# Smaller first modulation blocks, token tiles normed one by one, and a store's wait two tiles later, in a diffusion-trunk kernel

## The reference, cut to what matters

```python
mod = jax.nn.silu(cond) @ w_mod[l] + b_mod[l]          # cond = c_ctx or c; w_mod is 1024 x 6144
shift1, scale1, gate1, shift2, scale2, gate2 = jnp.split(mod, 6, axis=-1)
h = _rms_norm(x, g_pre_mix) * (1 + scale1) + shift1    # per token, over 1024 features
proj = jnp.einsum('bld,de->ble', h, w_in)              # 1024 -> 512 q, 128 k, 128 v, 512 gu, 512 gv
```

## Time and profile before

| | |
|---|---|
| median of 3 runs | 643.16 us (642.53 to 644.21) |
| profiled execution | 639.3 us |
| its span, first to last instruction | 637.4 us |
| TensorE busy | 539.1 us (85% of the span) |
| VectorE, ScalarE, GpSimd busy | 182.9, 150.7, 175.4 us |
| moved by the DMA engines | 173.21 MB, mean 272 GB/s |

### The profile page before, as it was taken

How to read it: one execution, slowest core, us unless ns; L and a number is a source line. 1 busy time by engine, 2 the same in 40 slices (tenths; PEclk the granted TensorE clock), 3 DMA queues, 4 the chain that set the end, 5 groups by cost and what they waited for, 6 DMA issues and landing times.

```text
span 637.4 us, 10100 instructions
## 1 busy us (share of the span) xinstructions
PE 539.1 (85%) x3527; PEld 308.3 (48%) x3527; DVE 182.9 (29%) x572; ACT 150.7 (24%) x375; POOL 175.4 (28%) x242
## 2 busy tenths in 40 slices
PE   0689999999989999999997899899997878878700
PEld 0644684454575664555553465565653434434300
DVE  1311160001348871344466211111111101111026
ACT  2511031012127870322221111112111111111133
POOL 1100000014404441344444333243333223320214
PEclk9999999999997999999996999999999888999955
DMA  8999626070499602441194999999999999999278
GB/s 295 360 369 386 229 66 229 0 263 1 139 257 408 256 2 95 169 166 64 50 347 156 343 407 407 406 408 402 400 398 401 382 400 394 406 408 407 84 310 199
DMA packets 57091, 173.21 MB, mean 272 GB/s; under 512 B 5756, under 2 KB 7476, under 8 KB 56128
## 3 DMA queue, kind: packets, MB, share of 16 engines
q1 hardware_dynamic: 48512, 153.76, 63.9%
q0 software_dynamic: 7184, 15.70, 7.8%
q10 hardware_dynamic: 1328, 2.87, 1.1%
HBM read 163.75 MB, written 16.68 MB: 283 GB/s over the span
## 4 chain that ended last, share of the span: by engine, by line
PE 54%; DMA 35%; DVE 4%; SPq 2%; issue 2%; ACT 1%; POOL 1%; POOLq 0%; ACTq 0%; DVEq 0%
DMA ring<-in_w_down_dram 15%; PE ps L746 11%; PE ps L639 11%; PE ps L518 7%; PE ps L596 5%; DMA w_6d<-in_w_down_dram 5%; PE ps L893 4%; PE ps L537 4%; DMA ring<-in_w_mod_dram 3%; PE ps L621 3%; PE ps L698 3%; DMA w_7d<-in_w_down_dram 3%; DMA w<-in_w_down_dram 3%; PE ps L723 2%; DMA ring<-in_w_up_dram 2%
## 5 line engine op out<-in xcount | busy, mean ns | idle before, releaser
L893 PE MATMUL ps<-ring,xt 128*64 128x256 f32 x704 | 83.6, 391 | 15.4 <-DMA ring<-in_w_up_dram 10.4
L893 PEld LDWEIGHTS ps<-ring,xt 128*64 128x64 f32 x704 | 55.4, 140 | 49.7 <-DMA ring<-in_w_up_dram 16.6
L639 PE MATMUL ps<-ring,h_t 128*128 128x512 f32 x160 | 69.5, 593 | 0.0
L1407 DVE TENSOR_TENSOR hid<-act_g,ps 128x128 f32<-128x128 f32 x32 | 9.2, 288 | 195.7 <-ACT act_g L1635 195.7
L893 PE MATMUL ps<-w,xt 128*64 128x256 f32 x416 | 50.9, 400 | 9.9 <-DMA w<-in_w_up_dram 7.9
L746 PE MATMUL ps<-ring,mix_t 128*128 128x512 f32 x120 | 53.6, 596 | 0.0
L1762 POOL DMA_INDIRECT expert_results<-y_sb,idx_out x32 | 32.7, 1021 | 60.3 <-ACT y_sb L1649 51.0
L893 PEld LDWEIGHTS ps<-w,xt 128*64 128x64 f32 x416 | 33.6, 144 | 31.6 <-DMA w<-in_w_up_dram 12.2
L639 PEld LDWEIGHTS ps<-ring,h_t 128*128 128x128 f32 x160 | 30.1, 190 | 36.8 <-issue 36.8
L1693 POOL TENSOR_TENSOR gm_stats<-gm_stats,half_pow 128x8 f32<-128x8 f32 x5 | 9.7, 1941 | 124.4 <-DVE gm_stats L1129 124.4
L1753 POOL DMA_INDIRECT xg<-h_rows,idx_in x32 | 33.4, 1043 | 28.2 <-POOL idx_in L1751 22.7
(11 more groups left out here) (242 smaller groups left out, 728.4 us busy)
## 6 DMA issues: line engine op xcount, KB each, us to landing
ring<-in_w_mod_dram SPq DMA_DIRECT2D x12, 2048.0 KB, 15.3
ring<-in_w_gate_dram SPq DMA_DIRECT2D x20, 1024.0 KB, 9.4
ring<-in_w_up_dram SPq DMA_DIRECT2D x20, 1024.0 KB, 14.2
ring<-in_w_down_dram SPq DMA_DIRECT2D x20, 1024.0 KB, 16.4
w<-in_w_gate_dram SPq DMA_DIRECT2D x12, 1024.0 KB, 8.3
w<-in_w_up_dram SPq DMA_DIRECT2D x12, 1024.0 KB, 13.5
y_back<-expert_results SPq DMA_DIRECT2D x5, 1024.0 KB, 9.0
ring<-in_w_in_dram SPq DMA_DIRECT2D x2, 2048.0 KB, 18.7
```

The source lines that it names most:

```text
L639: last = pe.matmul(ps[:, 4 + u % 4, :], h_t[:, k, i * P:(i + 1) * P], w[:, k, :], start=(k == 0), stop=(k == KC - 1))
L893: last = pe.matmul(bank[fh * SLOT:(fh + 1) * SLOT, 0:FE].rearrange("p (a f) -> p a f", a=2), x_t[:, k % 4, (k // 4) * SLOT:(k // 4 + 1) * ...
```

## The change

The first two blocks are cut anew: `m0` now has chunks 0 and 1 of both `shift1` and `scale1` (two transfers of 256 columns), and `m1` chunks 2 and 3 of both. So `m0` alone gives what query chunks 0 and 1 need. SyncE loads tile 0 and latent tile 1 first, then `cst`, the other tiles, `cst_once`, `m0`, the first half of the query weights, and only then `m1`. Means, `pow` and scaling go tile by tile, GpSimd doing five `pow` of one column; VectorE scales tiles 0, 1 and 2, ScalarE 3 and 4. Tiles 0, 1 and 2 are turned ahead of `m0`, and `m1` moves behind query chunk 0. The cached keys, cached values, sink logits and router weights are loaded by GpSimd after the query projection's end, beside the gating weights that it used to load after the last `turn_tokens`; the cached keys are turned in the `gv` stage. ScalarE waits for the stores of `new_k` and `new_v` at tile 2 instead of at tile 0.

```diff
-MB_FIRST = [0, 8, 4, 12] + list(range(16, N_MOD * KC, MB_CHUNKS))
+MB_PARTS = [[(0, 2), (8, 2)], [(2, 2), (10, 2)], [(4, 4)], [(12, 4)]] + [
+    [(j, 4)] for j in range(16, N_MOD * KC, MB_CHUNKS)]
...
+        DVE_CHUNKS, ACT_CHUNKS = [0, 2, 4, 5], [1, 3, 6, 7]
...
+            sp.dma_start(res[:, 0, :], x_prompt[0]).then_inc(s_xp, 16)
+            sp.dma_start(res[:, 1, :], x_lat[:, 0]).then_inc(s_xp, 16)
             sp.dma_start(cst[:], consts[:, 0:N_KEPT]).then_inc(s_const, 16)
+            sp.dma_start(res[:, 2:TILES, :], x_lat[:, 1:]).then_inc(s_xs, 16)
             sp.dma_start(cst_once[:], consts[:, N_KEPT:]).then_inc(s_const, 16)
-            sp.dma_start(res[:, 0, :], x_prompt[0]).then_inc(s_xp, 16)
-            sp.dma_start(res[:, 1:TILES, :], x_lat).then_inc(s_xs, 16)
...
             load_mod(0)
+            load_in("q", 0, ATT, slice(0, KC // 2), wide_in[place("q")])
             load_mod(1)
-            load_in("q", 0, ATT, slice(0, KC // 2), wide_in[place("q")])
...
-            pe.wait_ge(s_rows, 144)
-            transpose(ps[:, 3, 256:256 + N_ROWS], rows[:, :], N_ROWS)
-            transpose(ps[:, 3, 128:256], cache_sb[:, :]).then_inc(s_colps, 1)
-            pe.wait_ge(s_silu, 2)
+            pe.wait_ge(s_rows, 128)
+            transpose(ps[:, 3, 256:256 + N_ROWS], rows[:, :], N_ROWS).then_inc(s_colps, 1)
...
+            for i in range(3):
+                turn_tokens(i)
+            pe.wait_ge(s_silu, 2)
             mod_block(0)
-            turn_tokens(0)
+            turn_tokens(3)
             mod_turn(0)
-            turn_tokens(1)
-            mod_block(1)
-            turn_tokens(2)
-            mod_turn(1)
-            for i in range(3, TILES):
-                turn_tokens(i)
+            turn_tokens(4)
...
             queries(0, range(TILES))
-            queries(1, range(TILES))
+            mod_block(1)
+            queries(1, range(2))
+            mod_turn(1)
+            queries(1, range(2, TILES))
             mod_block(2)
...
                 mod_turn(5)
+                pe.wait_ge(s_cv, 48)
+                pe.wait_ge(qk_dve, TILES)
+                transpose(ps[:, 3, 128:256], cache_sb[:, :]).then_inc(s_colps, 1)
...
+            mean_token(2)
+            tokens_out(0)
+            mean_token(3)
+            scaled_token(2)
+            tokens_out(1)
+            mean_token(4)
+            tokens_out(2)
             mod_cols(0)
-            tokens_out(0)
+            tokens_out(3)
             mod_sum(0)
-            tokens_out(1)
+            tokens_out(4)
+            pre_mix(0)
             mod_cols(1)
-            tokens_out(2)
             mod_sum(1)
-            for i in range(3, TILES):
-                tokens_out(i)
-            pre_mix_half(0)
+            pre_mix(1)
...
                 if i == 2:
-                    act.wait_ge(s_newkv, 16)
+                    act.wait_ge(s_newkv, 32)
...
                     act.dma_start(new_v[0, 0].rearrange("s h d -> s (h d)"), v_all[:, 5, :]).then_inc(s_newkv, 16)
-                    act.wait_ge(s_newkv, 32)
...
+            for i in range(TILES):
+                pool.wait_ge(s_ms1, i + 1)
+                rsqrt(stats[:, 7, i:i + 1], stats[:, 1, i:i + 1], 1, s_rs1)
+
+            pool.wait_ge(ht_tr, TILES)
+            pool.wait_ge(qkv_mm, 1)
+            pool.dma_start(cache_sb[:, :], cache_k[0, 0].rearrange("s h d -> s (h d)")).then_inc(s_cv, 16)
```

More of the change, by code:

```diff
@@ L979, in _, with mean_token, scaled_token @@
             link(dve.memset(ones_b[:], 1.0))
+            def mean_token(i):
+                dve.wait_ge(s_sq1, i + 1)
+                dve.tensor_scalar(stats[:, 1, i:i + 1], stats[:, 0, i:i + 1], 1.0 / D, EPS, ALU.mult,
+                                  ALU.add).then_inc(s_ms1, 1)
+            def scaled_token(i):
+                dve.wait_ge(s_rs1, i + 1)
+                dve.tensor_scalar(res[:, i], res[:, i], stats[:, 7, i:i + 1], None, ALU.mult).then_inc(xn_dve, 1)
+            mean_token(0)
+            mean_token(1)
+            scaled_token(0)
+            dve.wait_ge(s_colps, 1)
+            dve.tensor_copy(cols[:], ps[:, 3, 256:256 + N_ROWS]).then_inc(s_cols, 1)
+            dve.wait_ge(s_cols, 1)
+            scaled_token(1)
             dve.wait_ge(s_const, 32)
@@ L1006, in mod_sum @@
                 dve.wait_ge(mod_tr, b + 1)
-                j0 = MB_FIRST[b]
-                bias = cols[:, ROWS["b_mod"][0] + j0:ROWS["b_mod"][0] + j0 + MB_CHUNKS]
-                dve.tensor_tensor(mod[:, j0:j0 + MB_CHUNKS, :],
-                                  ps[:, 2, 0:P].rearrange("p (g r) -> p g r", r=32)[:, :, 0:2],
-                                  bias.unsqueeze(2).broadcast_to((P, MB_CHUNKS, 2)), ALU.add).then_inc(mod_col, 1)
+                turned = ps[:, 2, 0:P].rearrange("p (g r) -> p g r", r=32)[:, :, 0:2]
+                at_ = 0
+                for j, n in MB_PARTS[b]:
+                    bias = cols[:, ROWS["b_mod"][0] + j:ROWS["b_mod"][0] + j + n]
+                    last = dve.tensor_tensor(mod[:, j:j + n, :], turned[:, at_:at_ + n],
+                                             bias.unsqueeze(2).broadcast_to((P, n, 2)), ALU.add)
+                    at_ += n
+                last.then_inc(mod_col, 1)
             def pre_cols(sub, gain):
@@ L1041, in pre_mix_half @@
                     dve.wait_ge(ht_act, TILES)
-                for k in range(4 * z, 4 * z + 2):
+                for k in [k for k in DVE_CHUNKS if k0 <= k < k0 + n]:
                     for cn, (a, b) in enumerate(((0, P), (P, TILES * P))):
@@ L1114, in _ @@
             mod_sum(5)
+            dve.wait_ge(s_colps, 2)
+            dve.tensor_copy(k_t[:, 0:P], ps[:, 3, 128:256]).then_inc(s_cols, 1)
+            dve.tensor_scalar(nsink[:], sink[:], -1.0, None, ALU.mult)
             def normed_values(i):
@@ L1469, in _, with token_squares @@
             act.dma_start(rows[ROWS["gm_b"][0]:ROWS["gm_b"][1], :], gm_b[0]).then_inc(s_rows, 16)
-            act.dma_start(cache_sb[:, :], cache_k[0, 0].rearrange("s h d -> s (h d)")).then_inc(s_rows, 16)
             act.wait_ge(s_zero, 1)
             act.activation(cond[:, 0, 0:2], cond[:, 0, 2:4], ACT.Silu).then_inc(s_silu, 1)
-            for i in range(TILES):
-                act.wait_ge(s_xp if i == 0 else s_xs, 16)
+            def token_squares(i):
                 if i:
@@ L1489, in _ @@
                          ps[:, 5 + 2 * (i % 2), :].rearrange("p (k q) -> p k q", q=P)).then_inc(ht_act, 1)
+            act.wait_ge(s_xp, 32)
+            token_squares(0)
+            token_squares(1)
+            act.wait_ge(s_cols, 1)
+            act.wait_ge(s_silu, 1)
+            act.activation(cond[:, :, 0:2], cols[:, 0:2 * KC].rearrange("p (c k) -> p k c", c=2),
+                           ACT.Silu).then_inc(s_silu, 1)
+            act.wait_ge(s_xs, 16)
+            token_squares(2)
+            tokens_out(0)
+            token_squares(3)
+            token_squares(4)
+            tokens_out(1)
+            scaled_token(3)
+            tokens_out(2)
+            scaled_token(4)
+            tokens_out(3)
+            tokens_out(4)
             act.wait_ge(ht_act, TILES)
             act.wait_ge(ht_dve, TILES)
-            for z in range(2):
+            for z, ks in enumerate(((1,), (3,), (6, 7))):
                 act.wait_ge(s_pre, z + 1)
-                for k in range(4 * z + 2, 4 * z + 4):
+                for k in ks:
                     for cn, (a, b) in enumerate(((0, P), (P, TILES * P))):
```

77 lines of the change are left out of this document (31 added, 46 removed).

## The result

The changed kernel takes 632.84 us (median of 4 runs, 630.05 to 635.53) against 642.85 us before (4 runs): a ratio of 0.984, 95% interval 0.981 to 0.987. The forecast was 637.0 us in a range of 634.8 to 640.9; the way was right, the gain of 10 us is larger than any that the range held. The profiled execution took 630.05 us with a span of 628.2 us; set against the 639.3 us of the profiled execution before, that is 9.25 us.

A forecast was written before the change was run, and what follows sets the result against it. The prediction took the chain from `m0`'s load through TensorE as the bound, a shorter head ending equally earlier. Keys and values 6.1 us earlier, about 0.1 us lost behind: 643.16 − 6.1 = 637.0 us, range 634.8 to 640.9.

The forecast's parts named there:

- the arrival of `m0`: First modulation block's load on SyncE's queue: lands at 19.3 us instead of 20.74, block starts at about 19.4 us.
- the way from there to the first query matmul: TensorE from the first block's start to the query projection: 7.0 us instead of 13.61, first query matmul at 26.4 us.
- dense stretch: TensorE from first query matmul to keys and values: 40.9 us instead of 38.95, since it takes `m1` in.
- the dip: Slow DMA windows from 4 to 10 us, 634 KB or 1.6 us short, taken as caused by the small loads.
- the bound: Earliest landing of `m0`: 18.5 us, if 1 KB rows cost nothing and some wait between engines goes too.
- My fast case: First block's start to first query matmul with TensorE at fast speed: 6.5 us, against 9.2 us at slow speed.
- The key and value stage, 0: Moving ScalarE's wait for the stores to tile 2 is worth 0, since TensorE has no hole in that stretch.
- Rival 1: Head: low DMA windows stay, `m0` used at 21.0 us, TensorE slow; 640.9 us; under 5 us off, chance 0.3.
- slow block: First modulation block at TensorE's slow speed, 3.64 us instead of 1.88; first query matmul 9.2 us after its start.
- rival 3: Head: getting tile 2 ready and turned, not `m0`'s load, holds the first block; 646 us if ending at 28.5; chance 0.04.
- ladder: Steps ahead of `m0` that load, square, scale and turn tile 2: done by 18.4 us, 1.0 us ahead of `m0`.

The follow-up runs named there:

- small loads late: Kernel before, with cached keys, cached values, sink logits and router weights loaded by GpSimd after the query projection, cached keys turned in the `gv` stage: 646.20 us.
- constants first: Changed kernel with both constant tables loaded ahead of the tiles on SyncE's queue again: 635.39 us.
- old cut: Changed kernel with the first two blocks cut as before (2 KB rows), the second block ahead of the query projection again: 636.18 us.
- sink first: Changed kernel with only the sink logits' broadcast load back at GpSimd's start: 635.20 us.
- wait at tile 0: Changed kernel with ScalarE waiting for both stores of new keys and values at tile 0 again: 639.28 us.
- loads after keys and values: Changed kernel with GpSimd's seven loads issued only after the keys and values of all tiles: 635.00 us.
- second table late: Changed kernel with the second constants table loaded behind the first block, and GpSimd's loads after the keys and values of all tiles: 635.30 us.

## Why the prediction was wrong

The mechanism held: the chain enters at `m0`, every step in front of the query projection counts, TensorE carries the gain on, and what the head wins the end has. The sizes were off, all to the same side but one. The steps that failed are two terms of the sum, both put too long: the arrival of `m0` (said 19.4 us, used at 17.77, 1.6 us) and the way from there to the first query matmul (said 7.0 us, measured 5.85, 1.15 us). Together they are 2.8 us, of which the dense stretch takes a little back: keys and values came 2.5 us earlier than forecast.

- **`m0` at 19.3 us.** It was used at 17.77. I took the dip's 1.6 us and 0.3 us of bytes; measured are 20.1 to 21.4 us in three executions with the old loads, 18.3 and 19.3 us with the small loads late, 18.42 us in the changed kernel with the constants first, and 17.7 to 17.8 us with the tiles first. The rows of 1 KB cost 0.6 us as forecast (the load landed at 17.64 us, with the old cut at 17.05). So the small loads were priced about right, at 1.9 us where the means give 2. The order of equal bytes was priced at nothing and is worth 0.65 us (17.77 against 18.42). What else brings the load from 18.2 to 19.2 us down to 17.05, at rows of 2 KB, stays open; in the prediction it is only in the bound ("some wait of one engine for another goes too"), without a price.
- **From `m0` to the first query matmul, 7.0 us.** Measured 5.85: block 1.96, tiles and turn 2.00, and a last hole of 1.89 us instead of 2.23. My fast case was 6.5 us, 0.35 us of it because I added up a turn and two tiles that overlap; I had taken 7.0 for a speed that would rise inside the block, and it had risen before it. The shorter hole is not from the smaller chunk count: the kernel before with the small loads late has four chunks and a hole of 1.90 us. There GpSimd doesn't issue its load of the gating weights in the hole. First the kernel before, then that one (start us, us):

```profile
32.54 0.94 POOL L1701 DMA_DIRECT2D ws_raw<-in_gm_ws_dram  x1 [11.57 <-PE ps L518]
32.89 0.56 DVE L1035 COPY pre<-mod 128x8 f32<-128x8 f32 x1
32.95 0.49 DVE L1036 SCALAR_TENSOR_TENSOR pre<-mod,cols 128x8 f32<-128x8 f32 x1
```

```profile
30.16 0.16 DVE L1034 COPY pre<-mod 128x8 f32<-128x8 f32 x1
30.23 0.16 DVE L1035 SCALAR_TENSOR_TENSOR pre<-mod,cols 128x8 f32<-128x8 f32 x1
```

The same two VectorE instructions take 0.56 and 0.49 us beside GpSimd's issue in all three executions that have it there, and 0.16 us each in the two without it. That the issue is the cause is argued from this, not tested alone.
- **The dense stretch, 40.9 us.** Measured 40.99. But that is the stretch of the kernel before as its first execution had it. The second has 1.7 us of low clock in it, which the profile that I worked from lacks. I set my sum against the profiled 639.3 us and shifted it to the median, 3.9 us higher, as if those 3.9 us lay in something that the change leaves alone. Where a run has that low clock, 1.7 us of them lie right behind the hole that the change shortens, and no execution of the changed kernel has it. How many runs have it is not known: of the kernel before only two executions have a profile.
- **The key and value stage, 0.** Right for the wait in the kernel before (0.999). Wrong for the pair: I priced the moved loads and the moved wait one by one, each at nothing. GpSimd's loads double the stores' landing, and together with the old wait they cost 5 to 6 us; with the new one, the stage stays 0.6 to 1.2 us longer than before. The prediction's sentence that at tile 2 the 4.3 us are almost over used a store's landing that the same change altered.
- **The rivals.** Rival 1 (dip and slow block stay) and rival 3 (ladder) did not come, but both are real: the slow block appears in four variants (3.29 to 3.64 us), the ladder ended only 0.3 us ahead of the load, and in two variants (old cut, sink first) tile 2 holds the block. That the forecast of a fast block came true is in part luck: no row of the kernel before showed that tiles ahead would make the block fast, and in three variants the same 25 transposes ahead were not enough.

In sum, from the two executions of each kernel: keys and values are 8.7 and 11.1 us earlier (73.27 to 64.61 and 75.80 to 64.67), block 4 8.1 and 9.9 us, the executions 9.25 and 10.35 us. The runs' medians over both timings are 633.4 us against 642.9, 9.5 us. What lies between 8.1 and 9.5 can be the low clock ahead of the query projection and the scatter behind block 4, where one kernel's executions differ by 2 us (509.66 and 511.69 us from block 4 to the last row of TensorE before, 508.81 and 511.26 after). How much of it is which stays open.

The Trainium skill ("TensorE: Matmul & The Clock Gate", Part 4) says that a transpose does not count as a busy TensorE in the same way and the fast clock does not engage for it. Here it does: with nothing but 17 transposes ahead of it, tile 2 is turned in 1.1 us instead of 1.97, and the block takes 1.96 us, in the changed kernel, its repeat and three variants (wait at tile 0, loads after keys and values, old cut); with one or two transposes ahead, the block takes 3.16 to 3.64 us. But transposes don't always do it in time: with the sink first and with the second table late the same 25 transposes leave the block at 3.29 and 3.64 us. So I was right not to follow the rule, and the trace gave no ground to count on the whole 1.7 us either. The Trainium skill's "DMA: Bandwidth & Descriptors" (Specifications), by which rows of 512 bytes and more run at line rate, disagrees with 349 GB/s for rows of 1 KB from 14 to 16 us, where the same engines move 386 GB/s with the rows of 2 KB of the old cut.

## What to carry to other kernels

When a change moves loads, price each transfer that is under way at the new place again, and then the waits on them: here the moved wait alone was worth nothing and the moved loads alone cost 0.4%, and together they gained 0.4%. When a stage's clock or hole differs between executions, one profile is a sample; take the sum against the execution it came from, but ask what in it the slower runs would have had. And work done in a wait can be worth more than its own length, if it leaves TensorE fast for what follows; how close to the edge that is, a profile of one execution doesn't say.

## What the hardware showed that I had not expected

- A broadcast of 32 bytes to 128 rows, 4 KB in all, issued at the start beside large loads, makes them land 1.5 us later (the first block's at 19.1 instead of 17.64 us), with windows of 215 and 270 GB/s where 400 were moved.
- Transposes can bring TensorE to its fast speed: the same block of 64 records takes 1.96 us behind 25 transposes in five executions and 3.64 us behind one. It is fragile: behind the same 25 transposes it took 3.64 us with a hole of 1.8 us between the second and the third tile, 3.29 us with a hole of 0.86 us there, while the five fast executions have 0.86 to 1.07 us, and 3.42 us where tile 2 was already fast (1.09 us) and the granted clock fell to 0.50 behind a hole of 1.24 us.
- Two small VectorE instructions took 0.56 and 0.49 us while GpSimd issued a load (0.94 us), and 0.16 us each without it.
- The two stores of 64 KB landed after 3.9 us before, and after 7.3 and 8.6 us beside seven loads of GpSimd's queue.
